# Sums of squares of the mixer's keys and queries: four reduced-precision products with high and low parts, one half later, for two plain float32 products

## What is computed

```python
proj = xn @ w_in
qkv, z, b_raw, a_raw, glu = jnp.split(proj, ...)
qkv = jax.nn.silu(causal_depthwise_conv(qkv, dn_conv_w))
q, k, v = jnp.split(qkv, 3, axis=-1)
q = l2_normalize(q.reshape(hd))        # x * rsqrt(sum(x*x) + EPS) over the 128 of a head
k = l2_normalize(k.reshape(hd))
```

## Time and profile before

| | |
|---|---|
| median of 3 runs | 2566.45 us (2566.37 to 2567.07) |
| profiled execution | 2566.27 us |
| its span, first to last instruction | 2564.5 us |
| busy: PE, DVE, ACT | 2543.6, 1674.9, 1339.4 us |
| mean granted clock of TensorE | 0.999 |

### The profile page before, as it was taken

The page is one execution under the profiler, slowest core; times in us unless marked ns, Lnnn a source line. Parts: engine busy times, 40 slices in busy tenths (PEclk is TensorE's granted clock), DMA queues, the critical chain, the costliest instruction groups (busy, mean ns, idle before and its releaser), DMA issues.

```text
span 2564.5 us, 33902 instructions
## 1 busy us (share of the span) xinstructions
PE 2543.6 (99%) x13816; PEld 2149.8 (84%) x13816; DVE 1674.9 (65%) x2150; ACT 1339.4 (52%) x1893; POOL 0.2 (0%) x4
## 2 busy tenths in 40 slices
PE   9999999999999999999999999999999999999998
PEld 7878888888888888887888888888888888888887
DVE  7686566655665566668778987555566655665565
ACT  6565554444444446568766656544554444444444
POOL 0000000000000000000000000000000000000000
PEclk9999999999999999999999999999999999999999
DMA  6544666566556555555454447554656655655654
GB/s 226 166 138 145 223 222 202 188 196 192 189 195 191 189 195 178 189 184 171 144 181 147 149 149 253 175 166 153 197 181 197 197 185 193 195 185 195 196 187 143
DMA packets 235858, 470.79 MB, mean 184 GB/s; under 512 B 8283, under 2 KB 17206, under 8 KB 234550
## 3 DMA queue, kind: packets, MB, share of 16 engines
q1 hardware_dynamic: 234950, 467.04, 55.7%
q10 hardware_dynamic: 752, 1.58, 0.2%
HBM read 462.30 MB, written 6.29 MB: 183 GB/s over the span
## 4 chain that ended last, share of the span: by engine, by line
PE 49%; DVE 1%; ACT 1%; issue 0%; DVEq 0%
PE ps L1291 10%; PE ps L1293 10%; PE ps L1292 10%; PE ps L1330 9%; PE ps L1329 5%; PE ps L1679 1%; PE ps L1362 0%; ACT WH L1911 0%; PE ps L1829 0%; PE ps L1857 0%; PE ps L1828 0%; PE ps L1856 0%; PE ps L1855 0%; PE ps L1827 0%; PE ps L1662 0%
## 5 line engine op out<-in xcount | busy, mean ns | idle before, releaser
L2663 DVE TENSOR_TENSOR WL<-Wt,WH 128x1024 fp32r<-128x1024 f32 (+1 forms) x861 | 1037.9, 1210 | 678.1 <-ACT WH L1911 630.0
L1911 ACT ACTIVATE WH<-Wt 128x1024 fp32r<-128x1024 f32 (+1 forms) x861 | 895.4, 1047 | 777.6 <-PE ps L1293 517.6
L1291 PE MATMUL ps<-WH,XT 128*128 128x512 f32 (+1 forms) x1184 | 469.6, 397 | 0.8 <-DVE WL L2663 0.5
L1293 PE MATMUL ps<-WH,XT 128*128 128x512 f32 (+1 forms) x1184 | 459.5, 388 | 0.0
L1292 PE MATMUL ps<-WL,XT 128*128 128x512 f32 (+1 forms) x1184 | 459.2, 388 | 0.0
L1291 PE MATMUL ps<-WH,HT 128*128 128x512 f32 (+2 forms) x1176 | 456.1, 388 | 1.5 <-DVE WL L2663 1.5
L1293 PE MATMUL ps<-WH,HT 128*128 128x512 f32 (+2 forms) x1176 | 451.4, 384 | 0.0
L1292 PE MATMUL ps<-WL,HT 128*128 128x512 f32 (+2 forms) x1176 | 451.0, 384 | 0.0
L1330 PE MATMUL ps<-XT,WH 128*128 128x512 f32 x960 | 336.5, 394 | 0.0
L1330 PE MATMUL ps<-HT,WH 128*128 128x512 f32 x960 | 336.5, 394 | 0.0
L1329 PE MATMUL ps<-XT,WL 128*128 128x256 f32 x960 | 266.6, 278 | 0.0
(11 more groups left out here) (424 smaller groups left out, 1922.2 us busy)
## 6 DMA issues: line engine op xcount, KB each, us to landing
Wt<-in_mlp_w SPq DMA_DIRECT2D x128, 1024.0 KB, 5.2
Wt<-in_w_up SPq DMA_DIRECT2D x64, 1024.0 KB, 5.2
Wt<-in_w_down SPq DMA_DIRECT2D x64, 1024.0 KB, 5.0
Wt<-in_w_in SPq DMA_DIRECT2D x53, 1024.0 KB, 5.1
Wt<-in_w_out SPq DMA_DIRECT2D x32, 1024.0 KB, 5.1
Wt<-in_xa_wk SPq DMA_DIRECT2D x16, 1024.0 KB, 5.1
Wt<-in_xa_wv SPq DMA_DIRECT2D x16, 1024.0 KB, 5.1
Wt<-in_xa_wq SPq DMA_DIRECT2D x16, 1024.0 KB, 5.2
```

The costliest lines, as they stand in the source:

```text
L1291: pe.matmul(o, xh, wh, start=start, stop=False)
L1293: done = pe.matmul(o, xl, wh, start=False, stop=stop)
L1911: act.activation(m.WH[:, i % NR, 0:2 * w], m.Wt[:, slot % NW, h * 2 * w:(h + 1) * 2 * w], ACT.Copy).then_inc(*up("wsplit.a", i))
L2663: dve.tensor_tensor(m.WL[:, i % NR, 0:2 * w], m.Wt[:, slot % NW, h * 2 * w:(h + 1) * 2 * w], m.WH[:, i % NR, 0:2 * w].bitcast(F32), SUB).t ...
```

## The change

`qk_square` gets two more instructions on ACT: at n = 0 a copy of the ones (128x128) to `ONR` in float32r, and at every n a copy of the squares (128x1024) to `QEH`, the high part. A new step `qk_low` on DVE subtracts it from the squares and puts the low part in `QEL`, which lies where `QE` lies. It has its own `yield`, so `qk_sum`, `qk_rsqrt` and `qk_scale` come one half later. `qk_sum` on PE waits for the low part, and for each 512 columns does two float32r products with the ones, of the high and of the low part. `QEH` and `ONR` lie in space that other tensors take later.

```diff
--- before.py
+++ after.py
@@ -256,6 +256,9 @@
         self.QC = arena("QC", [P, 4, 259], 4096)
         self.QA = [arena("QA0", [P, 4, 256], 17408), arena("QA1", [P, 4, 256], 59392)]
         self.QE = [arena("QE0", [P, 4, 256], 29696), arena("QE1", [P, 4, 256], 54272)]
+        self.QEL = [arena("QEL0", [P, 4, 256], 29696, F32R), arena("QEL1", [P, 4, 256], 54272, F32R)]
+        self.QEH = arena("QEH", [P, 4, 256], 50176, F32R)
+        self.ONR = arena("ONR", [P, P], 58368, F32R)
         self.QE2 = arena("QE2", [P, 2, 512], 29696)
         self.PRD = [arena(f"PRD{i}", [P, 4, 256], 63488 + 4096 * i) for i in range(2)]
         self.KTn = arena("KTn", [P, 8, 256], 33792)
@@ -923,6 +926,8 @@
             return
         p.do("qk_square", n)
         yield
+        p.do("qk_low", n)
+        yield
         p.do("qk_sum", n, *p.banks(2))
         yield
         p.do("qk_rsqrt", n)
@@ -1585,13 +1590,14 @@
 
     @named
     def qk_sum(n, *bs):
-        qe = m.QE[n % 2][:, :, :].rearrange("p c t -> p (c t)")
-        on.wait_ge(*at("qkv.a", "square", n))
+        hi, lo = (t[:, :, :].rearrange("p c t -> p (c t)") for t in (m.QEH, m.QEL[n % 2]))
+        on.wait_ge(*at("qkv.v", "square low", n))
         for pr, b in enumerate(bs):
+            cs = slice(pr * 512, (pr + 1) * 512)
             for s in freed(b):
                 on.wait_ge(*s)
-            pe.matmul(m.bank(b), m.cst("ones"), qe[:, pr * 512:(pr + 1) * 512],
-                      start=True, stop=True).then_inc(*up("qkv.t", "sum", n, pr))
+            pe.matmul(m.bank(b), m.ONR[:, :], hi[:, cs], start=True, stop=False)
+            pe.matmul(m.bank(b), m.ONR[:, :], lo[:, cs], start=False, stop=True).then_inc(*up("qkv.t", "sum", n, pr))
 
     @named
     def gates_sum(b):
@@ -2297,6 +2303,12 @@
         on.wait_ge(*at("qkv.v", "mul", n))
         act.activation(flat(m.QE[n % 2][:, :, :]), flat(m.QA[n % 2][:, :, :]), ACT.Square).then_inc(
             *up("qkv.a", "square", n))
+        if n == 0:
+            act.activation(m.ONR[:, :], m.cst("ones"), ACT.Copy).then_inc(*up("qkv.a", "ones"))
+        else:
+            on.wait_ge(*at("qkv.t", "sum", n - 1, 1))
+        on.wait_ge(*at("qkv.a", "square", n))
+        act.activation(flat(m.QEH[:, :, :]), flat(m.QE[n % 2][:, :, :]), ACT.Copy).then_inc(*up("qkv.a", "square high", n))
 
     @named
     def qk_sum(n, *bs):
@@ -3215,6 +3227,12 @@
         dve.tensor_tensor(qa, qa, qkv_exps(n), MUL).then_inc(*up("qkv.v", "mul", n))
 
     @named
+    def qk_low(n):
+        on.wait_ge(*at("qkv.a", "square high", n))
+        dve.tensor_tensor(flat(m.QEL[n % 2][:, :, :]), flat(m.QE[n % 2][:, :, :]), flat(m.QEH[:, :, :]).bitcast(F32), SUB
+                          ).then_inc(*up("qkv.v", "square low", n))
+
+    @named
     def qk_scale(kind, c, n):
         dst = flat((m.KTn if kind == "k" else m.QTn)[:, 4 * c:4 * c + 4, :])
         on.wait_ge(*at("qkv.a", "rsqrt", n))
```

## The result

The changed kernel takes 2576.95 us (median of 5 runs, 2576.22 to 2578.38), the kernel before 2566.45 beside it (median of 5 too): a ratio of 1.0041 with an interval of 1.0030 to 1.0052. It is slower by 10.5 us, more than the 0.2% that can be told from nothing. The forecast was 2573.4, range 2570.2 to 2577.0: the sign is right, the time lies at the very edge of the range, and 3.6 us of it are not in the sum.

A forecast was written before the change was run, and what follows sets the result against it. The prediction took PE (busy 2543.6 of 2564.5 us) to bound the kernel. Waits of 9.96 us plus 0.44 for slow first products less 3.36 saved gave +7.0 on 2566.27, with 0.18 for the median 2573.4; range 2570.2 to 2577.0.

The forecast's parts named there:

- signs of being right: Four PE waits of 2.3 to 2.7 us for QEL, products 0.23 apart, next half 1.7 to 1.8 later, later idle unchanged.
- signs of being wrong: First QEH product without a hole, PE's clock under 1.0 behind a place, or waits for WL at 1274 and 1280 gone.
- Cheap products: On PE, four reduced products of 0.91 us replace two plain ones of 1.75, saving 0.84 us a place.
- the order of the queues: ACT and DVE run strictly first in, first out, so QEL stands behind the WL split and AC's addition; sum +7.0 us.
- the move itself: The sums, logarithm, its exponential and the scaling of keys and queries come one half later, at no cost.
- The clock falls: Rival: waits bring PE back to 1.2 GHz, 4 us a place, 16 us more than the sum, 2589.4; chance 0.05.
- slower hand-offs: Upper end: each of three hand-offs a place, Square to QEH to QEL to PE, takes 0.24 us more; sum 9.9, 2576.3.
- What else moves, at nothing: Later logarithm and scaling, and ACT's added 1.0 us a place, fit into idle time or split lead and cost nothing.
- no wait at all: Rival: DVE has QEL ready when PE comes, only 3.4 us saved remains, 2563.0; chance 0.07 together with half a wait.
- The wait is given back: Rival: DVE and ACT gain lead, later PE waits near 1274 and 1280 shrink by 2.0 us, 2571.4, no change; chance 0.08.
- The new products are not cheap: Rival: reduced products with ones take 0.88 us like plain ones, 10.4 us more than the sum, 2583.8; chance 0.03.

The follow-up runs named there:

- the kernel with the filled wait: The changed kernel with 8 unused 512-column products on PE in front of each wait for the low part: 2573.28 us, ratio 1.0027.
- the kernel with all the work: The changed kernel's copies and subtraction kept, but PE sums by plain products one half later without waiting for them: 2570.69 us, ratio 1.0016.
- the waits of 1.5 us: The changed kernel with the low-part subtraction moved into the Square's step, sums still two halves behind the Square: 2573.07 us, ratio 1.0026.
- the longer wait: The changed kernel with one more DVE instruction of 128x1024 in front of the low part: 2582.58 us, ratio 1.0061.
- the fast kernel above: The kernel before with Square writing float32r, one reduced product per 512 columns, and DVE evicting both blocks to QB in chunks 4 to 9: 2562.41 us.

## Why the prediction was right, and where it fell short

**The mechanism and its size.** QEL stands behind WL and AC on DVE, and PE stands still for it. Forecast per place: 2.62, 2.61, 2.45 and 2.28 us; measured from start to start 2.45, 2.38, 2.41 and 2.38, 9.6 in place of 9.96 in all. The whole was 7.0 us; the kernel with the filled wait measured 6.8, and the places without a fall 1.7 each. Of the prediction's signs of being right, the idle times for QEL, the products 0.23 us apart and the later idle times came out; the next half 1.7 to 1.8 us later did at two places of four. One of its signs of being wrong came out too, PE's clock under 1.0 behind a place.

**Its terms.** ONR moved QEH by less than was taken: QEH starts 1.16 us behind the start of the Square with ONR between them and 1.09 without (1193.05 less 1191.96, second place), so 0.07 and not 0.2, since ONR runs while QEH would wait for the Square's end. QEH moved WH by 0.95 (0.96), the hand-off from DVE to PE was 0.05 (0.05). The four new products take 1.04 us from the first to the next half (forecast 0.91 and 0.11), so plain products at 1.75 are 0.7 dearer with the slow first one counted. Cheap products and the order of the queues are as forecast. That the move itself is free holds (1.0000).

**The term that was mis-sized.** "The clock falls" stood among the rivals, with 0.05, as something that happens at all four places or at none, for 4 us each. It happened at two of four, for 3.41 us and about 1.5 us of time each, beside the wait: 3.1 us that belonged in the sum as a likely addition. That the time lies inside the range all the same is luck: the range had no room for falls, its end at 2577.0 came from slower hand-offs, which did not occur (0.05 us from QEL to PE), and four of the ten executions of the change lie above it. I had set the longest idle time with a full clock behind it, 1.61 us, against waits of 2.3 to 2.6 and given the row too much weight: nothing in it spoke for waits that are longer. The price was far too high: I took it from the start of the run, where nothing says that the low clock lasts as long as behind a wait. The Trainium skill ("TensorE: Matmul & The Clock Gate", "What's actually happening") has it that an idle stretch can bring 1.2 GHz back; the second and the fourth place agree with it, and the waits of 3.5 us with 1.00 behind them show that it need not. The rest of the difference to 2576.95 lies at the start of the run: the two profiled executions of the change were 0.75 and 0.41 us behind at the half before the first place (1164.63 in the first; 1167.02 against 1166.61 in the other), ahead of anything that was changed.

**The step that was wrong.** "What else moves, at nothing" put ACT's and DVE's added work at zero beside PE. For ACT's copies alone it holds (1.0001). For DVE it does not: its subtraction costs 3.0 us alone, and 4.2 were measured with the copies, when PE does not wait for it. This hid in the sum because PE stood still for the same instruction at the same time, and one price covered the other. It comes out in the rival "no wait at all", priced at 2563.0: a kernel with this work has a floor near 2570, an estimate from the 25.62 us a chunk of the kernel with all the work; no run has that work, the cheap products and no wait. With the sums a half later still it was not even that, since that edit put two more instructions into the chain (27.71 us a chunk). The rows that would have told stood in the trace: each engine's own pace over a chunk, 24.44 us for PE, and for the pair the same, held by PE by so little that 24.37 is its own. I read the busy shares and one place, and took DVE's 1.83 us and ACT's 2.02 us of idle time for room; they are the times that the two wait for each other.

**The other rivals.** "The wait is given back" is refuted: the later waits of PE (1.15, 0.37 and 0.90 us) are as they were, since ACT and DVE move along with PE; ACT's eviction waits for PE after every place. "The new products are not cheap" is refuted by their distance of 0.23 us.

**What stays open.** What decides whether a wait is followed by a fall. In the profiled executions lengths do not order it (waits for QEL: 2.0 us three of three, 1.5 none of three, 2.2 four of eight, 3.5 one of four; for QA 1.83 with a fall, and 1.83, 1.85, 1.85 and 1.87 without), and it comes at the same two places in both profiled executions of the change. Three of the eight executions with the waits of 1.5 us have a mean clock of 0.998, so falls may occur there too, without more time. What a fall costs where the chain between ACT and DVE sets the time is known only from two kernels: nothing. The slowest run of the longer wait, 2585.4, would need more falls of 1.5 us than it has places, and its mean clock, 0.995, says the same; where they lie is not on record. Which single link of the chain between ACT and DVE is the tightest was not taken apart beyond the eviction. A version with both parts of the squares on the shorter chain was not tried: the fast kernel above leaves out what float32r loses of a square, so it shows where the time is, and does not replace either kernel as it stands.

## What to carry to other kernels

Before cheapening the busiest engine, measure the pace of the others per round of the loop, start to start of one marked instruction: if two engines that wait for each other are within 1% of the busiest one, cheaper work there gives next to nothing (5.2 us of PE's work gave 1.2, which is not clear of noise). An instruction more in the chain between the two costs nearly its length in each round (DVE's subtraction, 1.14 us from start to start, cost 0.95); one that falls into idle time need not (ACT's copies alone cost nothing). An operand made one half ahead is only as early as the queue in front of it, so count what stands there before moving a consumer. And price an idle hole of some 2 us in TensorE's stream with a possible fall of the clock on top, as a term with a chance and not as a case apart.

## What the hardware showed that I had not expected

- Behind waits of PE of 1.8 to 3.6 us the granted clock fell to 0.50 in some cases only, each time for 3.41 us in the record, at about 1.5 us of time in the changed kernel, and at none in two others, where PE would have waited later anyway. Fillers of 1.8 us in the wait took the falls away.
- A copy of 128x128 on ACT lasts 0.29 us, and the next instruction follows after 0.20: a fifth of the 0.95 that 128x1024 takes. It delayed what stood behind it by only 0.07 us, since it ran while that waited anyway.
- Work that only one engine does can be cheaper on the busier of two: the eviction moved from ACT to DVE saved 3.0 us, since it left the part of the chain in which the other engine waited.
